# Six stationary buffers moved to six different offsets modulo 512 bytes

## The chip, the cores and the metric

The kernel runs on one core of one Trainium2 chip. The metric is the device time of one execution in microseconds; less is better. TensorE (PE) multiplies matrices, VectorE (DVE), ScalarE (ACT) and GpSimd (POOL) work element by element, and SyncE (SP) issues most of the loads from device memory.

## The reference

Two decoder layers act on x of 256 tokens by 2048 features, in float32. Layer 0 mixes tokens by gated linear attention, layer 1 by softmax attention with a forget gate, and both end in a SwiGLU network. In short:

```
for i in range(DEPTH):                       # DEPTH = 2
    h = rms_norm(x, norm_mix[i])
    x = x + (gla_mixer if i == 0 else fox_mixer)(h, ...)   # h @ w_in, mixing, (...) @ w_o
    h = rms_norm(x, norm_ffn[i])
    x = x + (silu(h @ w_gate) * (h @ w_up)) @ w_down       # 2048 -> 5632 -> 2048
```

Nearly all of the arithmetic lies in the products of 256 token rows with large weight matrices, which are read from device memory once.

## The kernel before

**The split.** Each float32 operand of a large product is split into a high part and a low part, both of type float32r. A product is then the sum of three: high by high, high by low, low by high. The weights stream in as chunks of 256 rows by 512 columns: `raw` receives the chunk by DMA, ScalarE writes `w_hi` from it (line 551), VectorE writes `w_lo` (line 890). Each of these three is a ring of 4 slots.

**The stationary buffers.** The activations are transposed and stand in pairs: `xt_hi` and `xt_lo` (the normed x, 16 blocks of 128 features by 256 tokens), `ht_hi` and `ht_lo` (the inner SwiGLU activations, 44 blocks) and `yt_hi` and `yt_lo` (a mixer's output, 16 blocks). One block holds 1024 bytes on each partition, and a matmul takes half of it, 128 tokens or 512 bytes, as its stationary operand. The weights are the moving operand, 512 columns or 2048 bytes. This is the inner loop of `tile`, lines 328 to 337:

```
for r in range(KC_CHUNK):                                     # 2
    k = j * KC_CHUNK + r
    wh = w_hi[:, slot, r * N:(r + 1) * N]                     # N = 512
    wl = w_lo[:, slot, r * N:(r + 1) * N]
    for b in range(TB):                                       # 2
        xh, xl = hi[:, k, b * P:(b + 1) * P], lo[:, k, b * P:(b + 1) * P]
        pe.matmul(o, xh, wh, start=(k == 0), stop=False)      # L335
        pe.matmul(o, xh, wl, start=False, stop=False)         # L336
        last = pe.matmul(o, xl, wh, start=False, stop=...)    # L337
```

There are 816 chunks of 12 such matmuls each. The trace names a matmul `acc<-w_hi,xt_hi`: it writes `acc` in PSUM and reads those two tensors. The weight load of the stationary operand is a separate instruction, LDWEIGHTS, with a row of its own ("PEld"). The second argument of `pe.matmul` is the stationary operand, the third the moving one.

**The narrow products.** Once in each layer, `narrow_product` multiplies the normed x with 16 further columns of the input weights, and there the roles are turned round: the stationary operand is a window of 128 columns into a narrow weight array, and x is the moving operand with 256 columns.

```
for k in range(KC):                                           # 16
    wh, wl = hi[:, k * R:k * R + P], lo[:, k * R:k * R + P]   # R = 16
    pe.matmul(wk[:, 0, 0:S], wh, xt_hi[:, k, :], ...)         # L347
    pe.matmul(wk[:, 0, 0:S], wh, xt_lo[:, k, :], ...)         # L348
    last = pe.matmul(wk[:, 0, 0:S], wl, xt_hi[:, k, :], ...)  # L349
```

**Where things lie.** A first pad brings `xres` to a multiple of 2048 bytes, and `xres`, `xt_hi`, `xt_lo`, `raw`, `w_hi` and `w_lo` follow without gaps, each 16384 bytes long, so all of them begin at multiples of 2048. Then come small tensors, and from `base`, again a multiple of 2048, a region in which the mixers' tensors and `ht`, `yt` take turns (function `at`, with offsets in units of 1024 bytes).

**The order of work.** Each engine's program is written out by hand, and semaphores join them. On TensorE the tiles follow one another; transposes of activations (line 305) and the small products of the mixers (lines 435 to 515) are slipped in between chunks. Nothing in this order depends on addresses.

Of the kernel before, what the change touches and what calls it, by code (L numbers as in the profile page):

```python
# [31 lines left out]
F32R = mybir.dt.float32r  # L32
# [5 lines left out]
P = 128  # L38
# [37 lines left out]
def build(nc, x, norm_mix, norm_ffn, gla_w_in, gla_w_g2, gla_b_g2, gla_o_gain, gla_w_o,  # L76
          fox_w_in, fox_b_f, fox_q_gain, fox_k_gain, fox_w_o, w_gate, w_up, w_down, out):
    S, D = x.shape[1], x.shape[2]
    KC = D // P
# [4 lines left out]
    HC = DFF // P  # L84
# [31 lines left out]
    with ctx:  # L116
        def sb(name, shape, dt=F32):
            return ctx.enter_context(nc.sbuf_tensor(name, shape, dt))
# [3 lines left out]


        ALIGN = 2048
        sb("pad", [P, (-(-(-nc.sbuf_base // 32) * 32)) % ALIGN // 4])
        xres = sb("xres", [P, TB, D])
        xt_hi = sb("xt_hi", [P, KC, S], F32R)
        xt_lo = sb("xt_lo", [P, KC, S], F32R)
        raw = sb("raw", [P, SLOTS, KC_CHUNK * N])
        w_hi = sb("w_hi", [P, SLOTS, KC_CHUNK * N], F32R)  # L130
        w_lo = sb("w_lo", [P, SLOTS, KC_CHUNK * N], F32R)
# [17 lines left out]
        ohr = sb("o_rstd", [P, GH, TB])  # L149


        base = -(-nc.sbuf_base // ALIGN) * ALIGN
        room = [0]

        def at(name, shape, offset, dt=F32):
            size = 4 * int(np.prod(shape[1:]))
            room[0] = max(room[0], offset + size)
            return nc.alloc_sbuf_tensor_at(name, shape, dt, offset=base + offset)
        K = 1024
        ht_hi = at("ht_hi", [P, HC, S], 0, F32R)  # L160
        ht_lo = at("ht_lo", [P, HC, S], 44 * K, F32R)
        yt_hi = at("yt_hi", [P, KC, S], 0, F32R)
        yt_lo = at("yt_lo", [P, KC, S], 16 * K, F32R)

        qT = at("gla_qT", [P, GF, S], 0)
        kT = at("gla_kT", [P, GF, S], 8 * K)
# [1249 lines left out]
```

## Time and profile before

| | |
|---|---|
| median of 3 runs | 2388.08 us (2388.03 to 2390.64) |
| the profiled execution | 2389.47 us, of which the span from first to last instruction is 2387.8 us |
| PE busy | 2364.1 us, 99% of the span, 10882 matmuls |
| weight loads (PEld) busy | 1965.7 us, 82% |
| DVE, ACT, POOL busy | 1256.1 us, 1070.0 us, 156.9 us |
| mean granted TensorE clock | 0.999 of full speed |

Matmuls overlap in the array, and their ends are modelled. So a row's duration of one matmul (some 390 ns) is longer than the distance between two starts; the distance is what an added matmul costs, and it is read from start times.

### The profile page before, as it was taken

The page shows a single profiled execution, that of the slowest core. Times are in us where ns is not written, and L with a number is a line of the kernel's source. Part 1 is how long each engine was busy: PE and PEld are TensorE (multiplying, and loading weights), DVE is VectorE, ACT ScalarE, POOL GpSimd, SP SyncE. Part 2 cuts the span into 40 slices and gives each one's busy share as a digit, 9 for nine tenths or more (in the row PEclk, how much of TensorE's full clock was granted, in tenths as well). Part 3 has the DMA queues.
Part 4 walks back from the last instruction along what each step waited for, and adds up shares of the span by engine and source line. Part 5 has one row for each costly group of instructions (what it writes and reads, how often), then busy time and mean ns, then how long its engine had stood idle before and what let it go on. Part 6 is the DMA issues. An engine that isn't in the chain of part 4 may idle for free.

```text
span 2387.8 us, 30464 instructions
## 1 busy us (share of the span) xinstructions
PE 2364.1 (99%) x10882; PEld 1965.7 (82%) x10882; DVE 1256.1 (53%) x1210; ACT 1070.0 (45%) x1242; POOL 156.9 (7%) x188
## 2 busy tenths in 40 slices
PE   8999999999999999999999999999999999999999
PEld 6788878888888888888888888888888888888887
DVE  4668655555445454444465555555454454444443
ACT  5544555444444444444444455444444444444332
POOL 2213210000000000000011110000000000000000
PEclk9999999999999999999999999999999999999999
DMA  6455455565665655566878786655665665656664
GB/s 206 133 168 159 143 166 185 189 191 184 193 193 181 193 189 186 193 190 188 195 165 185 179 212 162 157 176 189 192 190 187 191 191 187 188 182 196 206 200 138
DMA packets 228184, 435.39 MB, mean 182 GB/s; under 512 B 17444, under 2 KB 17544, under 8 KB 227992
## 3 DMA queue, kind: packets, MB, share of 16 engines
q1 hardware_dynamic: 223040, 429.97, 60.9%
q0 software_dynamic: 752, 4.21, 0.5%
q10 hardware_dynamic: 4328, 0.37, 0.1%
q8 instruction: 38, 0.62, 0.1%
q14 instruction: 26, 0.21, 0.0%
HBM read 432.38 MB, written 2.11 MB: 182 GB/s over the span
## 4 chain that ended last, share of the span: by engine, by line
PE 98%; DVE 1%; ACT 0%; DMA 0%; issue 0%; POOL 0%; DVEq 0%; ACTq 0%
PE acc L335 31%; PE acc L337 31%; PE acc L336 31%; PE tp L305 2%; PE wk L435 1%; DVE w_lo L890 1%; PE wk L487 0%; PE tp L497 0%; DMA xres<-in_x_dram 0%; PE wk L409 0%; PE wk L348 0%; PE wk L349 0%; PE wk L347 0%; PE wk L513 0%; PE wk L515 0%; PE wk L514 0%
## 5 line engine op out<-in xcount | busy, mean ns | idle before, releaser
L890 DVE TENSOR_TENSOR w_lo<-raw,w_hi 128x1024 fp32r<-128x1024 f32 x816 | 1029.9, 1272 | 885.9 <-ACT w_hi L551 885.3
L551 ACT ACTIVATE w_hi<-raw 128x1024 fp32r<-128x1024 f32 x816 | 861.0, 1060 | 1020.8 <-PE acc L337 956.1
L335 PE MATMUL acc<-w_hi,xt_hi 128*128 128x512 f32 x2304 | 907.4, 394 | 6.4 <-DVE gla_kT L1020 3.1
L337 PE MATMUL acc<-w_hi,xt_lo 128*128 128x512 f32 x2304 | 899.1, 390 | 0.0
L336 PE MATMUL acc<-w_lo,xt_hi 128*128 128x512 f32 x2304 | 898.6, 390 | 0.0
L335 PEld LDWEIGHTS acc<-w_hi,xt_hi 128*128 128x128 f32 x2304 | 433.7, 188 | 97.8 <-issue 5.6
L337 PEld LDWEIGHTS acc<-w_hi,xt_lo 128*128 128x128 f32 x2304 | 433.4, 188 | 90.7
L336 PEld LDWEIGHTS acc<-w_lo,xt_hi 128*128 128x128 f32 x2304 | 433.9, 188 | 89.0 <-issue 1.0
L335 PE MATMUL acc<-w_hi,ht_hi 128*128 128x512 f32 x704 | 274.6, 390 | 0.0
L337 PE MATMUL acc<-w_hi,ht_lo 128*128 128x512 f32 x704 | 274.2, 389 | 0.0
L336 PE MATMUL acc<-w_lo,ht_hi 128*128 128x512 f32 x704 | 274.1, 389 | 0.0
L337 PEld LDWEIGHTS acc<-w_hi,ht_lo 128*128 128x128 f32 x704 | 132.2, 188 | 27.5
L335 PEld LDWEIGHTS acc<-w_hi,ht_hi 128*128 128x128 f32 x704 | 132.2, 188 | 27.2
L336 PEld LDWEIGHTS acc<-w_lo,ht_hi 128*128 128x128 f32 x704 | 132.2, 188 | 27.1
L335 PE MATMUL acc<-w_hi,yt_hi 128*128 128x512 f32 x256 | 100.5, 393 | 0.0
L337 PE MATMUL acc<-w_hi,yt_lo 128*128 128x512 f32 x256 | 99.8, 390 | 0.0
L336 PE MATMUL acc<-w_lo,yt_hi 128*128 128x512 f32 x256 | 99.7, 389 | 0.0
L1305 POOL COPY xres<-stage 128x1024 f32<-128x1024 f32 x12 | 12.5, 1042 | 1067.9 <-DVE stage L923 1067.9
L305 PEld LDWEIGHTS tp<-ident,stage 128*128 128x128 f32 x432 | 50.3, 140 | 8.9 <-issue 2.0
L305 PE MATMUL tp<-ident,stage 128*128 128x128 f32 x432 | 56.0, 273 | 1.6 <-DVE stage L981 1.6
L337 PEld LDWEIGHTS acc<-w_hi,yt_lo 128*128 128x128 f32 x256 | 48.1, 188 | 10.0
L336 PEld LDWEIGHTS acc<-w_lo,yt_hi 128*128 128x128 f32 x256 | 48.1, 188 | 9.7
(173 smaller groups left out, 888.8 us busy)
## 6 DMA issues: line engine op xcount, KB each, us to landing
raw<-in_ffn_w_gate_dram SPq DMA_DIRECT2D x176, 512.0 KB, 4.3
raw<-in_ffn_w_up_dram SPq DMA_DIRECT2D x176, 512.0 KB, 4.3
raw<-in_ffn_w_down_dram SPq DMA_DIRECT2D x176, 512.0 KB, 4.5
raw<-in_fox_w_in_dram SPq DMA_DIRECT2D x128, 512.0 KB, 5.5
raw<-in_gla_w_in_dram SPq DMA_DIRECT2D x96, 512.0 KB, 4.1
raw<-in_gla_w_o_dram SPq DMA_DIRECT2D x32, 512.0 KB, 4.5
raw<-in_fox_w_o_dram SPq DMA_DIRECT2D x32, 512.0 KB, 4.5
xres<-in_x_dram SPq DMA_DIRECT2D x4, 512.0 KB, 7.9
```

Of the source, the lines that this page charges most:

```text
L305: last = pe.transpose(tp[:, kk, b * P:(b + 1) * P], src[:, b, kk * P:(kk + 1) * P], ident[:, :])
L335: pe.matmul(o, xh, wh, start=(k == 0), stop=False)
L336: pe.matmul(o, xh, wl, start=False, stop=False)
L337: last = pe.matmul(o, xl, wh, start=False, stop=(k == chunks * KC_CHUNK - 1))
L435: last = pe.matmul(wk[:, b, h * P:(h + 1) * P], ks, qs, start=(kf == 0), stop=(kf == FPH - 1))
L551: nc.scalar.activation(w_hi[:, slot, :], raw[:, slot, :], ACT.Copy).then_inc(hi_done, 1)
L890: nc.vector.tensor_tensor(w_lo[:, slot, :], raw[:, slot, :], w_hi[:, slot, :].bitcast(F32), ALU.subtract).then_inc(lo_done, 1)
L1305: nc.gpsimd.tensor_copy(xres[:, :, t * N:(t + 1) * N], stage[:, :, :]).then_inc(x_saved, 1)
```

## The change

The stationary buffers no longer begin at multiples of 512 bytes but at six different offsets modulo 512: `xt_hi` 64, `xt_lo` 256, `ht_hi` 128, `ht_lo` 320, `yt_hi` 192, `yt_lo` 448. `xres` stays where it was. `raw`, `w_hi` and `w_lo` move by 2048 bytes and stay at multiples of 2048. `base` becomes the next multiple of 512 instead of 2048, which moves the mixers' tensors by 512 bytes. No instruction is added, removed or reordered: on each of the five engines the program has the same rows in the same order, with other addresses.

```
         ALIGN = 2048
-        sb("pad", [P, (-(-(-nc.sbuf_base // 32) * 32)) % ALIGN // 4])
+        XT_HI_AT, XT_LO_AT = 64, 256
+        HT_HI_AT, HT_LO_AT = 128, 320
+        YT_HI_AT, YT_LO_AT = 192, 448
+
+        def to(name, align, offset):
+
+            start = -(-nc.sbuf_base // 32) * 32
+            gap = (offset - start) % align
+            if gap:
+                sb(name, [P, gap // 4])
+        to("pad_xres", ALIGN, 0)
         xres = sb("xres", [P, TB, D])
+        to("pad_xt_hi", 512, XT_HI_AT)
         xt_hi = sb("xt_hi", [P, KC, S], F32R)
+        to("pad_xt_lo", 512, XT_LO_AT)
         xt_lo = sb("xt_lo", [P, KC, S], F32R)
+        to("pad_raw", ALIGN, 0)
         raw = sb("raw", [P, SLOTS, KC_CHUNK * N])
         w_hi = sb("w_hi", [P, SLOTS, KC_CHUNK * N], F32R)
         w_lo = sb("w_lo", [P, SLOTS, KC_CHUNK * N], F32R)
...
-        base = -(-nc.sbuf_base // ALIGN) * ALIGN
+        base = -(-nc.sbuf_base // 512) * 512
...
         K = 1024
-        ht_hi = at("ht_hi", [P, HC, S], 0, F32R)
-        ht_lo = at("ht_lo", [P, HC, S], 44 * K, F32R)
-        yt_hi = at("yt_hi", [P, KC, S], 0, F32R)
-        yt_lo = at("yt_lo", [P, KC, S], 16 * K, F32R)
+        ht_hi = at("ht_hi", [P, HC, S], HT_HI_AT, F32R)
+        ht_lo = at("ht_lo", [P, HC, S], 44 * K + HT_LO_AT, F32R)
+        yt_hi = at("yt_hi", [P, KC, S], YT_HI_AT, F32R)
+        yt_lo = at("yt_lo", [P, KC, S], 16 * K + YT_LO_AT, F32R)
```

## Rows read from the trace of the kernel before

**Rows 1.** the page: busy time by engine, then the granted clock in 40 slices.
```profile
PE 2364.1 (99%) x10882; PEld 1965.7 (82%) x10882; DVE 1256.1 (53%) x1210; ACT 1070.0 (45%) x1242; POOL 156.9 (7%) x188
...
PEclk9999999999999999999999999999999999999999
```

**Rows 2.** the page: the chain that ended last, by engine, by line.
```profile
PE 98%; DVE 1%; ACT 0%; DMA 0%; issue 0%; POOL 0%; DVEq 0%; ACTq 0%
PE acc L335 31%; PE acc L337 31%; PE acc L336 31%; PE tp L305 2%; PE wk L435 1%; DVE w_lo L890 1%; PE wk L487 0%; PE tp L497 0%; DMA xres<-in_x_dram 0%; PE wk L409 0%; PE wk L348 0%; PE wk L349 0%; PE wk L347 0%; PE wk L513 0%; PE wk L515 0%; PE wk L514 0%
```

**Rows 3.** the page: TensorE by line (busy, mean ns of one | idle before).
```profile
L335 PE MATMUL acc<-w_hi,xt_hi 128*128 128x512 f32 x2304 | 907.4, 394 | 6.4 <-DVE gla_kT L1020 3.1
...
L336 PE MATMUL acc<-w_lo,xt_hi 128*128 128x512 f32 x2304 | 898.6, 390 | 0.0
L335 PEld LDWEIGHTS acc<-w_hi,xt_hi 128*128 128x128 f32 x2304 | 433.7, 188 | 97.8 <-issue 5.6
...
L335 PE MATMUL acc<-w_hi,ht_hi 128*128 128x512 f32 x704 | 274.6, 390 | 0.0
...
L335 PE MATMUL acc<-w_hi,yt_hi 128*128 128x512 f32 x256 | 100.5, 393 | 0.0
```

**Rows 4.** whom TensorE waited for: total us, times, longest.
```profile
PE tp L305 <- DMA xres<-in_x_dram: 5.5, 1, 5.5
PE tp L305 <- DVE xt_lo L931: 4.6, 1, 4.6
PE acc L335 <- DVE gla_kT L1020: 3.1, 1, 3.1
PE acc L335 <- DVE w_lo L890: 3.1, 2, 2.5
```

**Rows 5.** line 336 in three unbroken stretches: count, then first and last start.
```profile
L336 PE MATMUL acc<-w_lo,xt_hi x64: 386/389/390, 1974.2 to 2017.1; 128*128 128x512 f32 x64
...
L336 PE MATMUL acc<-w_lo,yt_hi x32: 387/390/391, 357.7 to 378.8; 128*128 128x512 f32 x32
...
L336 PE MATMUL acc<-w_lo,ht_hi x310: 388/389/390, 2159.9 to 2370.0; 128*128 128x512 f32 x155
```

**Rows 6.** timeline, first narrow product: start us, us, instruction.
```profile
39.81 0.28 PE L347 MATMUL wk<-xt_hi,gla_wn_hi 128*128 128x256 f32 x1
...
40.16 0.28 PE L347 MATMUL wk<-xt_hi,gla_wn_hi 128*128 128x256 f32 x1
...
40.52 0.28 PE L347 MATMUL wk<-xt_hi,gla_wn_hi 128*128 128x256 f32 x1
...
40.87 0.28 PE L347 MATMUL wk<-xt_hi,gla_wn_hi 128*128 128x256 f32 x1
...
41.23 0.28 PE L347 MATMUL wk<-xt_hi,gla_wn_hi 128*128 128x256 f32 x1
...
41.58 0.28 PE L347 MATMUL wk<-xt_hi,gla_wn_hi 128*128 128x256 f32 x1
...
41.94 0.28 PE L347 MATMUL wk<-xt_hi,gla_wn_hi 128*128 128x256 f32 x1
...
42.30 0.28 PE L347 MATMUL wk<-xt_hi,gla_wn_hi 128*128 128x256 f32 x1
...
42.65 0.28 PE L347 MATMUL wk<-xt_hi,gla_wn_hi 128*128 128x256 f32 x1
...
43.01 0.28 PE L347 MATMUL wk<-xt_hi,gla_wn_hi 128*128 128x256 f32 x1
...
45.14 0.28 PE L347 MATMUL wk<-xt_hi,gla_wn_hi 128*128 128x256 f32 x1
```

**Rows 7.** pieces of the chain: start us, us, what.
```profile
8.82 1.57 ACT xt_hi L595 x4
10.49 1.67 DVE xt_lo L931 x4
...
149.99 3.57 PE wk L435 x32
```

## The prediction

> **What bounds the kernel now.** I read the page from the top. TensorE is busy for 99% of the span and its granted clock is full, the upper of its two levels (2.4 GHz), in all slices [rows 1]. Such a busy share proves little, because the ends of matmuls are modelled. So I turn next to the chain of work that ended last: 98% of it is TensorE, and three lines of the inner loop, 335, 336 and 337, hold 31% each [rows 2]. No other engine decides anything for long. The list of TensorE's waits confirms it: the longest are 5.5 us for the first piece of x, 4.6 us for `xt_lo`, and twice 3.1 us in the first layer [rows 4], 16.3 us in all. The kernel is a stream of matmuls, and its time is their number times the distance from one start to the next.
>
> The number comes from the code, 816 chunks of 12, and from the rows by line: each of the three lines ran 2304 times with `xt`, 704 times with `ht` and 256 times with `yt` [rows 3], and 3 x 3264 is 9792. The distance comes from stretches in which nothing is slipped between the chunks. Line 336 is every third matmul there. With `xt` 64 of them lie between 1974.2 and 2017.1 us, so 42.9 / 63 / 3 = 227.0 ns a matmul; with `yt` 32 lie in 21.1 us, 226.9 ns; with `ht` 310 lie in 210.1 us, 226.6 ns [rows 5]. I take 226.8 ns. All three kinds pay the same within the rounding of the starts, and 9792 x 226.8 ns is 2220.8 us, 93% of the span of 2387.8 us. The rest, 167.0 us, is transposes, the mixers' small products and the waits.
>
> One nanosecond on each of these matmuls is 9.8 us, or 0.41%. About 0.2% (4.8 us) is what a measurement of this kernel can tell from no change, and that is 0.49 ns a matmul. The question is thus a fine one: does the address of the stationary operand move that distance by half a nanosecond?
>
> **What could be there to gain.** The narrow products, with 256 columns, start every 118.4 ns (worked out below). So 256 more columns cost 108.4 ns, 0.423 ns each, which is about one cycle of 2.4 GHz (0.417 ns). 512 such cycles are 213.3 ns, the distance is 226.8, and so 13.5 ns a matmul is something else. If the weight load and the moving stream got in each other's way, and if that depended on both starting at multiples of 512 bytes, this is where the change would act. The weight load takes 188 ns [rows 3] and so lies within the distance of 226.8 ns, beside the matmul before it. An offset that made only the load shorter would be covered by the 38.8 ns between the two, and bring nothing. An offset that made it longer would bring nothing either up to those 38.8 ns.
>
> **What the trace of before already tried.** The narrow product is the same experiment, on a small scale. Its stationary windows begin at k times 64 bytes in an array that begins at a multiple of 2048, so k = 0 to 7 run through all eight multiples of 64 modulo 512, the changed kernel's 64, 128, 192, 256, 320 and 448 among them. Its moving operand begins at a multiple of 512, as the ring does. Three matmuls make a step k. From the start of k = 0 to the start of k = 8 the steps of line 347 are 0.35, 0.36, 0.35, 0.36, 0.35, 0.36, 0.36 and 0.35 us, the next is 0.36, and 15 steps take 5.33 us [rows 6]: 355.3 ns a step, 118.4 ns a matmul. No residue stands out. If leaving the multiple of 512 took away most of the 13.5 ns, the steps between k = 0 and k = 8 would be up to 40 ns shorter than those at k = 0 and 8. They are not, by 10 ns in three matmuls, or 3.3 ns in one.
>
> The two kinds of product give the fixed part as well. At 0.423 ns a column, 512 columns take 216.8 ns of the 226.8, which leaves 10.0 ns. At one cycle of 2.4 GHz a column the fixed parts are 13.5 ns in the large products and 118.4 - 106.7 = 11.7 ns in the narrow ones. Either way a matmul whose stationary operand is off the multiple of 512 pays nearly all of what an aligned one pays.
>
> **The change part by part.**
> - The offsets of `xt`, `ht` and `yt` as stationary operands: 9792 matmuls. The value taken is 0 ns, since the eight residues of the narrow product cannot be told apart. The bound of the gain is the difference of the fixed parts, 1.8 ns or 17.6 us. The bound of the loss is the spread of the narrow steps, 3.3 ns or 32.6 us.
> - The ring moves by 2048 bytes and keeps its place modulo 2048: 0. Its slots already differ by 4096 bytes, and the matmuls keep their pace over all four.
> - `xt` as the moving operand of the narrow products, now off the multiple of 512: 96 matmuls. If each lost the whole fixed part of 10.0 ns again, it would be 1.0 us. Taken as 0.
> - The mixers' tensors move by 512 bytes. Their blocks already lie at 512-byte steps from each other; 32 small products of line 435 over such blocks take 3.57 us [rows 7], 111.6 ns each, and the groups of that line have all steps in them. Taken as 0; a tenth of it, for the 272 of that line, would be 3.0 us.
> - ScalarE's and VectorE's writes into the six buffers begin elsewhere. They are hidden behind TensorE, as these engines are busy 45% and 53% of the span [rows 1], except for the start, where four of `xt_hi` (1.57 us) and four of `xt_lo` (1.67 us) stand in the chain [rows 7], once more before the first chunk. If they took a tenth more or less, that would be 0.6 us. Taken as 0.
> - `yt_lo` now reaches 448 bytes into what follows it. The program's waits are the same, and the tensors there are used at other times, so nothing comes later.
>
> The sum is 0. The profiled execution took 2389.47 us, 1.67 us more than its span; the median of the runs is 1.39 us below it, and with no change the forecast is that median, **2388.1 us**.
>
> **Two pages weighed.** The 226.8 ns of [rows 5] stand against a page's figure. The Trainium skill, "TensorE: Matmul & The Clock Gate", section "Wait — 56ns, not 53.3ns?", gives 215.7 ns for back-to-back matmuls of 512 columns at the full clock. If the offsets brought this kernel there, the time would be an estimated 2388.1 - 9792 x 11.1 ns = 2279 us by that page. The trace does not agree with that figure here. The Trainium skill, "SBUF — State Buffer", section "Who interferes with whom", speaks against any such gain: TensorE has two independent read ports, one for the moving operand and one for the weight load, so the two have nothing to collide on. By that rule the time stays at 2388.1 us, and the even steps of [rows 6] agree.
>
> **The rivals.**
> - *Slower, by straddling.* An aligned 512-byte stationary operand lies within one block of 512 bytes; at an offset it lies in two. If the array's load then delays each matmul by a little, all 9792 pay. For it: the first narrow step, which begins with an aligned operand, takes 0.35 us and the mean step 355.3 ns, 5.3 ns in three or 1.8 ns in one. Against it: steps of 0.35 us come back at k = 2, 4 and 7, and the weight load has 38.8 ns of cover. Price: 9792 x 1.8 ns = 17.6 us, 2405.7 us; by the bound of 3.3 ns, 2420.7 us. It decides from 0.49 ns a matmul.
> - *Faster a little.* The fixed part falls from 13.5 to the narrow product's 11.7 ns. For it: that difference is in the rows. Against it: those matmuls have 256 columns, and the difference may come from that. Price: 17.6 us, 2370.5 us; half of it, 2379.3 us.
> - *Faster by much.* There is a collision, which the narrow product does not leave either, because `wn` and `x` share something else. Price: the fixed part of 10.0 ns at most, 97.9 us, 2290.2 us. Against it: even steps over all residues.
>
> **How the numbers follow.** No change has a chance of 0.64, slower by straddling 0.20, faster a little 0.12, faster by much 0.04. Within the first, the time is 2388.1 us give or take 4.8 us, 2383 to 2393. The two small rivals are steps of about one nanosecond or less as easily as of 1.8, so the range takes in half of each: down to the 2379 us of half the small gain, and up to 1.2 ns of loss, 2400 us. What is left out is the large gain, 0.04, a part of the small one, 0.05, and the losses above, 0.09.
>
> **What would show it.** Line 336 in the same stretches must again have 226.6 to 227.0 ns from start to start; a weight load of 188 ns that changed while the distance did not would prove the cover. Steps of the narrow product must stay at 355 ns. `xt`, `ht` and `yt` have different offsets, so if one residue matters, the three will part: that would make the prediction wrong in a way the three stretches show at once. A common shift of all three by more than 0.5 ns would refute it as well.

## The result and the profile after

The changed kernel is slower: 2437.2 us median (2437.0 to 2438.7) against 2388.06 us, a ratio of 1.0205 with a 95% interval of 1.019 to 1.022, or 49 us. The forecast was no change, 2388.1 us, in a range of 2379 to 2400.

The page of the changed kernel: busy times, granted clock, chain by engine, then TensorE by line. Its inner loop stands 13 lines lower, at 348 to 350.

```profile
PE 2413.1 (99%) x10882; PEld 1963.5 (81%) x10882; DVE 1255.8 (52%) x1210; ACT 1070.7 (44%) x1242; POOL 156.7 (6%) x188
...
PEclk9999999999999999999999999999999999999999
...
PE 98%; DVE 1%; ACT 0%; DMA 0%; issue 0%; POOL 0%; DVEq 0%; ACTq 0%
...
L348 PE MATMUL acc<-w_hi,xt_hi 128*128 128x512 f32 x2304 | 916.4, 398 | 4.9 <-DVE w_lo L903 3.4
...
L349 PE MATMUL acc<-w_lo,xt_hi 128*128 128x512 f32 x2304 | 909.6, 395 | 0.0
L348 PEld LDWEIGHTS acc<-w_hi,xt_hi 128*128 128x128 f32 x2304 | 433.0, 188 | 109.6 <-DVE w_lo L903 4.5
```

Against [rows 1] and [rows 2] nothing but TensorE's busy time has grown, by 49.0 us; clock and chain are the same. The weight load still takes 188 ns, as in [rows 3]. What has risen is the modelled duration of one matmul, from 394 to 398 ns on the first line and from 390 to 395 on the second. TensorE's waits (total us, times, longest) are no longer either:

```profile
PE tp L318 <- DMA xres<-in_x_dram: 5.6, 1, 5.6
PE tp L318 <- DVE xt_lo L944: 4.6, 1, 4.6
PE acc L348 <- DVE w_lo L903: 3.4, 3, 2.5
...
PE acc L348 <- DVE gla_kT L1033: 1.5, 1, 1.5
```

These four are 15.1 us, against 16.3 us in [rows 4]. So no wait has come in. What has changed is seen in unbroken stretches of line 349, the middle matmul of three: count, then first and last start in us. The first two are `xt`, in a late SwiGLU and in the first layer's projections (the product with `w_in`), then come `yt` and `ht`.

```profile
L349 PE MATMUL acc<-w_lo,xt_hi x63: 390/390/397, 1785.9 to 1829.3; 128*128 128x512 f32 x63
...
L349 PE MATMUL acc<-w_lo,xt_hi x32: 396/397/398, 86.3 to 107.8; 128*128 128x512 f32 x32
...
L349 PE MATMUL acc<-w_lo,yt_hi x31: 388/388/388, 385.0 to 405.6; 128*128 128x512 f32 x31
...
L349 PE MATMUL acc<-w_lo,ht_hi x351: 388/394/394, 2187.6 to 2429.1; 128*128 128x512 f32 x176
```

By the same working as for [rows 5]: 43.4 us / 62 / 3 is 233.3 ns from start to start for `xt`, 21.5 us / 31 / 3 is 231.2 ns in the projections, `yt` has 20.6 / 30 / 3 or 228.9 ns, and `ht` 241.5 / 350 / 3 or 230.0 ns. Before, all had 226.7, in ns. Of the changed kernel's 33 stretches of `xt` with 60 matmuls or more, 29 run at 233.3 ns, and four, three of them in the first layer's projections, at 231.1. The 49 us are there. Summed over all matmuls of the two traces, from start to start, those with `xt` took 40.9 us more, those with `ht` 7.0 us (2112 x 3.3 ns) and those with `yt` 1.7 us (768 x 2.2 ns), 49.5 us together. TensorE's few pauses came out 2.1 us shorter, nothing else moved by more than 0.2 us, and the span grew by 47.5 us.

A closer look, at the timeline of single matmuls in the projections (start us, modelled duration, instruction):

```profile
60.11 0.39 PE L348 MATMUL acc<-w_hi,xt_hi 128*128 128x512 f32 x1
60.34 0.40 PE L349 MATMUL acc<-w_lo,xt_hi 128*128 128x512 f32 x1
60.57 0.39 PE L350 MATMUL acc<-w_hi,xt_lo 128*128 128x512 f32 x1
60.80 0.39 PE L348 MATMUL acc<-w_hi,xt_hi 128*128 128x512 f32 x1
61.03 0.40 PE L349 MATMUL acc<-w_lo,xt_hi 128*128 128x512 f32 x1
61.26 0.39 PE L350 MATMUL acc<-w_hi,xt_lo 128*128 128x512 f32 x1
61.50 0.39 PE L348 MATMUL acc<-w_hi,xt_hi 128*128 128x512 f32 x1
```

Two rounds of three matmuls take 1.39 us (60.11 to 61.50), 231.7 ns each within the rounding, and the middle one of each three is modelled at 0.40 us where its neighbours have 0.39. It is a settled rhythm, not a scatter of delays: in ns the distances repeat 226, 236, 232 in the projections, and in the SwiGLU stages a pattern of six with a mean of 233.3. Written in cycles of 2.4 GHz the mean distances are 544 before and 554.7, 560, 549.3 and 552 after: thirty-four steps of 16 cycles before, and 34 2/3, 35, 34 1/3 and 34 1/2 after. What is whole is the pattern: three matmuls take 104 or 103 steps, six take 210 or 207. A step of 16 cycles is 6.67 ns, an estimated 16 columns at the 0.423 ns a column of the prediction, and 16 columns are 64 bytes on a partition.

### The profile page after: what moved, and what is told of

Same layout as the page of the kernel before. It is cut to its first block, busy times and chain, and to the rows that moved or that the text cites. A ratio compares the mean times of both kernels' runs of the same rounds, so it can differ in the third digit from the quotient of the medians.

```text
span 2435.3 us, 30464 instructions
## 1 busy us (share of the span) xinstructions
PE 2413.1 (99%) x10882; PEld 1963.5 (81%) x10882; DVE 1255.8 (52%) x1210; ACT 1070.7 (44%) x1242; POOL 156.7 (6%) x188
## 4 chain that ended last, share of the span: by engine, by line
PE 98%; DVE 1%; ACT 0%; DMA 0%; issue 0%; POOL 0%; DVEq 0%; ACTq 0%
PE acc L350 31%; PE acc L348 31%; PE acc L349 31%; PE tp L318 2%; PE wk L448 1%; DVE w_lo L903 1%; PE wk L500 0%; PE tp L510 0%; DMA xres<-in_x_dram 0%; PE wk L422 0%; PE wk L361 0%; PE wk L360 0%; PE wk L362 0%; PE wk L527 0%; PE wk L528 0%; PE wk L526 0%
## 5 line engine op out<-in xcount | busy, mean ns | idle before, releaser
L350 PE MATMUL acc<-w_hi,xt_lo 128*128 128x512 f32 x2304 | 912.3, 396 | 0.0
L349 PE MATMUL acc<-w_lo,xt_hi 128*128 128x512 f32 x2304 | 909.6, 395 | 0.0
```

The source lines that it names most:

```text
L350: last = pe.matmul(o, xl, wh, start=False, stop=(k == chunks * KC_CHUNK - 1))
```

## Experiments

In all of them the order of instructions is that of the kernel before, TensorE writes to the same places in PSUM, and a weight load takes 188 to 189 ns. Three kinds of matmul (`xt`, `ht`, `yt`) can have different offsets, so one kernel tries three at once. "Offset" is a place in bytes modulo 2048 for `xt` and the ring (all of `raw`, `w_hi`, `w_lo`, unless said otherwise), and modulo 512 for the others. The distance from start to start is worked out as above; with starts rounded to 0.1 us it is good to 0.5 ns for `xt`, 1 ns for `yt` and 0.1 ns for `ht`, and where this text gives a number of steps of 16 cycles or speaks of a settled distance, it is from the trace's starts in ns, after the first 24 matmuls of a stretch. The diffs are against the changed kernel and leave out its own lines; where two kernels share one, the second's values stand behind it. Where there is one timed run, its time is given as it stands: the kernel before, run beside them, took 2387.9 to 2391.0 us.

**Are equal offsets free?** (e1, against the changed kernel)

```
-        XT_HI_AT, XT_LO_AT = 64, 256
-        HT_HI_AT, HT_LO_AT = 128, 320
-        YT_HI_AT, YT_LO_AT = 192, 448
+        XT_HI_AT, XT_LO_AT = 64, 64
+        HT_HI_AT, HT_LO_AT = 256, 256
+        YT_HI_AT, YT_LO_AT = 128, 128
```

> High and low part of a pair at the same offset modulo 512: xt 64 and 64, ht 256 and 256, yt 128 and 128; ring at multiples of 2048. Theory A (each stationary operand that is off the multiple of 512 costs by itself, by crossing a boundary): all three kinds stay above the 226.7 ns from start to start of the kernel before, at 229 to 234 ns, and the time stays at 2410 to 2440 us. Theory B (what costs is that the two parts of a pair have different offsets, so that successive weight loads begin differently): all three return to 226.7 ns, time 2388 us. Theory C (what counts is the offset from the moving operand's): as A, with three different distances.

Measured: 2435.53 us, ratio 1.0195 (1.0178 to 1.0212). Line 349 with `xt`, `yt` and `ht`:

```profile
L349 PE MATMUL acc<-w_lo,xt_hi x63: 394/394/394, 1788.0 to 1831.4; 128*128 128x512 f32 x63
...
L349 PE MATMUL acc<-w_lo,yt_hi x31: 390/393/404, 387.1 to 408.0; 128*128 128x512 f32 x31
...
L349 PE MATMUL acc<-w_lo,ht_hi x351: 389/389/395, 2189.6 to 2427.6; 128*128 128x512 f32 x176
```

`xt` has 43.4 / 62 / 3, 233.3 ns; `yt` 232.2 (settled at 232.4); `ht`, with 238.0 us from first to last start, 238.0 / 350 / 3 or 226.7 ns. Theory B falls: equal parts at 64 and at 128 pay as much as unequal ones, and those of `xt` alone bring most of the loss of the changed kernel. Theory A falls in its plain form too, because 256 is free.

**Only one part moved** (e3)

```
+        XT_HI_AT, XT_LO_AT = 64, 0
+        HT_HI_AT, HT_LO_AT = 0, 64
+        YT_HI_AT, YT_LO_AT = 256, 512
```

> Only one part of each pair is off the multiple of 512: xt 64 and 0, ht 0 and 64, yt 256 and 0 (at 512). Two of three matmuls load the high part, one the low part. Theory A: the cost goes with the number of matmuls off the multiple, so xt and yt lose twice what ht loses; with some 6.6 ns a matmul for a full pair of xt, xt 231 ns and ht 229 ns. Theory B (a change of offset between successive loads costs): xt and ht lose alike, since both change offset twice in three matmuls. Time 2410 to 2425 us by either.

Measured: 2437.58 us. Two stretches with `xt`, then `yt`, then `ht`:

```profile
L349 PE MATMUL acc<-w_lo,xt_hi x63: 397/397/398, 453.3 to 496.3; 128*128 128x512 f32 x63
...
L349 PE MATMUL acc<-w_lo,xt_hi x63: 390/390/397, 1785.3 to 1828.7; 128*128 128x512 f32 x63
...
L349 PE MATMUL acc<-w_lo,yt_hi x31: 389/389/389, 385.0 to 405.4; 128*128 128x512 f32 x31
...
L349 PE MATMUL acc<-w_lo,ht_hi x351: 388/392/392, 2187.0 to 2429.6; 128*128 128x512 f32 x176
```

`xt` has 231.2 ns in one stretch and 233.3 in another, `ht` 231.0 (settled at 231.1), `yt` 226.7. One part off is nearly as dear as both, so the cost does not go with the number of matmuls off the multiple, as A had it. And matmuls with the same operand addresses can settle in two rhythms. They are the two of `xt` in the changed kernel, 231.1 and 233.3 ns: its offsets there, 64 and 256, are those of this run, 64 and 0, if 256 counts as 0.

**Does it matter where in 2048?** (e4)

```
+        XT_HI_AT, XT_LO_AT = 512, 1024      # xt pads modulo 2048
+        HT_HI_AT, HT_LO_AT = 0, 1024        # base is 512 modulo 2048
+        YT_HI_AT, YT_LO_AT = 512, 1024
```

> All six at multiples of 512 but at different places modulo 2048: xt 512 and 1024, ht 512 and 1536, yt 1024 and 1536. Theories A, B and C, which all count modulo 512: 226.7 ns for all, 2388 us, as the blocks of a buffer lie at steps of 512 in the kernel before too. A theory D, by which the pad to 2048 matters: above 226.7 ns in at least one kind, over 2395 us.

Measured: 2387.84 us, the time before. With `xt` 226.9 ns, with `ht` 226.7:

```profile
L349 PE MATMUL acc<-w_lo,xt_hi x63: 387/389/389, 447.5 to 489.7; 128*128 128x512 f32 x63
...
L349 PE MATMUL acc<-w_lo,ht_hi x351: 389/389/389, 2141.9 to 2379.9; 128*128 128x512 f32 x176
```

So the larger footprint, the ring 2048 bytes further on and the mixers' tensors 512 bytes further on, all of which this kernel shares with the changed one, cost nothing. The whole 49 us come from the offsets below 512.

**The stationary's address, or its distance from the ring?** (e2 and e7)

```
+        XT_HI_AT, XT_LO_AT = 0, 0           # e2          e7: 192, 192
+        HT_HI_AT, HT_LO_AT = 64, 64         #                  0, 0
+        YT_HI_AT, YT_LO_AT = 128, 128       #                 64, 64
-        to("pad_raw", ALIGN, 0)
+        to("pad_raw", ALIGN, 64)            #                 192
...
+        to("pad_stage", 512, 0)             # both
```

> The ring (raw, w_hi, w_lo) begins at 64 modulo 2048; xt at 0 and 0, ht at 64 and 64, yt at 128 and 128. Theory A (offset of the stationary operand alone): xt 226.7 ns from start to start, ht and yt above it, about 2395 to 2405 us. Theory C (offset of the stationary from the moving operand): ht, which lies as far from the ring as before, has 226.7 ns, while xt and yt are above, about 2420 to 2435 us. Theory B (unequal parts): 226.7 ns in all three, 2388 us.

Measured: 2408.84 us. `xt`, `yt` and `ht`:

```profile
L350 PE MATMUL acc<-w_lo,xt_hi x63: 388/388/388, 1768.6 to 1811.2; 128*128 128x512 f32 x63
...
L350 PE MATMUL acc<-w_lo,yt_hi x31: 393/398/398, 384.3 to 405.3; 128*128 128x512 f32 x31
...
L350 PE MATMUL acc<-w_lo,ht_hi x351: 389/389/389, 2162.9 to 2400.9; 128*128 128x512 f32 x176
```

> Ring at 192 modulo 2048, xt at 192 and 192, ht at 0 and 0, yt at 64 and 64. Theory C256 (offset from the ring counts): xt, off every multiple of 256 but level with the ring, has the 226.7 ns of the kernel before; ht, aligned but 64 above the ring modulo 256, has 233.3; yt, 128 from it, some 233. Time about 2403 us. Theory A (the stationary operand's own address counts): xt 228.9 ns, ht 226.7, yt 233.3, about 2405 us; the two differ by which kind pays.

Measured: 2406.04 us. `xt`, `yt` and `ht`:

```profile
L350 PE MATMUL acc<-w_lo,xt_hi x63: 389/389/395, 1762.4 to 1804.6; 128*128 128x512 f32 x63
...
L350 PE MATMUL acc<-w_lo,yt_hi x31: 390/393/404, 380.6 to 401.5; 128*128 128x512 f32 x31
...
L350 PE MATMUL acc<-w_lo,ht_hi x351: 393/398/398, 2153.1 to 2398.1; 128*128 128x512 f32 x176
```

These two runs separate A from C. In the first, `ht` stands off every multiple of 256 and is free (238.0 / 350 / 3 = 226.7 ns), because the ring is moved as far; `xt`, aligned but 64 below the ring, pays 229.0 ns. In the second, `xt` at 192 is level with the ring and has 226.9 ns, and `ht`, perfectly aligned, pays 233.3 ns. Theory C holds, in so far as the place against the ring counts, and theory A is dead. That `raw` moves with the ring is not the reason: in e8, below, `w_lo` alone is moved, and aligned `yt` goes from 226.7 to 232 ns.

**Modulo what, and how much for each offset?** (e5 and e6; ring at 0)

```
+        XT_HI_AT, XT_LO_AT = 192, 192       # e5          e6: 224, 224
+        HT_HI_AT, HT_LO_AT = 32, 32         #                 96, 96
+        YT_HI_AT, YT_LO_AT = 320, 320       #                160, 160
```

> Pairs at equal offsets, ring at multiples of 2048: xt 192, ht 32, yt 320. Theory C256 (the offset of the stationary from the moving operand counts modulo 256, as 0 gave 226.7 ns, 64 and 128 some 233, -64 gave 228.9 and 256 gave 226.7): yt at 320 behaves as 64, 233.3 ns; xt at 192 behaves as -64, 228.9 ns; ht at 32, not measured before, between 226.7 and 233.3. Theory C512 (modulo 512, and 256 is free by chance): yt at 320 = -192 and xt at 192 have distances of their own, not 233.3 and 228.9. Time by C256 about 2400 to 2410 us.

Measured: 2420.47 us. `xt`, `yt` and `ht`:

```profile
L349 PE MATMUL acc<-w_lo,xt_hi x63: 388/388/388, 1773.4 to 1815.9; 128*128 128x512 f32 x63
...
L349 PE MATMUL acc<-w_lo,yt_hi x31: 393/393/398, 383.0 to 404.0; 128*128 128x512 f32 x31
...
L349 PE MATMUL acc<-w_lo,ht_hi x351: 395/396/396, 2167.5 to 2412.5; 128*128 128x512 f32 x176
```

> Pairs at equal offsets, ring at multiples of 2048: xt 224 (that is -32 modulo 256), ht 96, yt 160. Theory C256 with a cost that falls back evenly beyond 128: xt between 226.7 and 228.9 ns, yt between 228.9 and 233, ht 233. A rival: there is an offset below the aligned one's 226.7 ns, which is two 16-cycle steps above 512 cycles; then xt, at -32, is the place for it, with 220 ns, and the time falls under 2370 us.

Measured: 2451.65 us. `xt`, `yt` and `ht`:

```profile
L349 PE MATMUL acc<-w_lo,xt_hi x63: 393/396/397, 1796.1 to 1839.5; 128*128 128x512 f32 x63
...
L349 PE MATMUL acc<-w_lo,yt_hi x31: 388/394/394, 387.0 to 408.0; 128*128 128x512 f32 x31
...
L349 PE MATMUL acc<-w_lo,ht_hi x351: 392/397/400, 2197.7 to 2443.7; 128*128 128x512 f32 x176
```

By its rows `xt` has 228.5 ns, within the rounding of the 229.0 in e2. The offset 320 gives the 233.3 ns of 64, and 192 the 229 of -64 in e2, as 256 gave the 226.7 of 0 in e1: the count is modulo 256 wherever it was tried. The guess that the cost falls back evenly beyond 128 is wrong, since 160 and 224 cost 233.3 ns as 64 does. So is the hope for a place below the aligned one. With both parts alike, and the offset counted from the ring modulo 256, these are the settled distances, with the number of matmuls after which the pattern of distances repeats:

| offset from the ring | ns from start to start | steps of 16 cycles | repeats after | from |
|---|---|---|---|---|
| 0 (also 256) | 226.7 | 34 | 1 | e1, e2, e3, e4, e7, e10 |
| 32 | 233.3 | 35 | 2 | e5 |
| 64 (also 320) | 233.3 | 35 | 1 or 2 | e1, e2, e5, e7 |
| 96 | 234.3 | 35 1/7 | 7 | e6 |
| 128 | 232.4 | 34 6/7 | 7 | e1, e7 |
| 160 | 233.3 | 35 | 3 | e6 |
| 192 (-64) | 228.9 | 34 1/3 | 3 | e2, e5 |
| 224 | 233.3 | 35 | 4 | e6 |

The kernel before has 226.7 ns as well, its single distances scattered between 225 and 228 ns. The rhythm of a row is that of most of its stretches, not of all: one stretch of `xt` in the first projections of e5, at 192, ran at 233.3 ns.

The changed kernel's `yt`, 192 and 448, is two times 192 by this count, and its 228.9 ns are those of the table.

**A version that keeps all at multiples of 256** (e10)

```
+        XT_HI_AT, XT_LO_AT = 256, 0
+        HT_HI_AT, HT_LO_AT = 256, 512
+        YT_HI_AT, YT_LO_AT = 768, 1280
-        to("pad_raw", ALIGN, 0)
+        to("pad_raw", 512, 0)
         raw = sb("raw", [P, SLOTS, KC_CHUNK * N])
+        to("pad_w_hi", 512, 0)
         w_hi = sb("w_hi", [P, SLOTS, KC_CHUNK * N], F32R)
+        to("pad_w_lo", 512, 256)
```

> Everything that TensorE reads in the large products begins at a multiple of 256 bytes, and no two the same way modulo 2048 if it can be had: xt 256 and 512, ht 1792 and 0, yt 256 and 768, w_hi 512, w_lo 768. Theory C256: 226.7 ns for all three kinds and the time of the kernel before, 2388 us, within 0.2%. Theory C512 or a rule of 2048: one or more kinds above 228 ns and over 2395 us.

Measured: 2388.27 us, ratio 1.000 (0.9991 to 1.001). `xt`, `yt` and `ht`, all at 226.7 to 226.9 ns:

```profile
L351 PE MATMUL acc<-w_lo,xt_hi x63: 387/389/389, 449.3 to 491.5; 128*128 128x512 f32 x63
...
L351 PE MATMUL acc<-w_lo,yt_hi x31: 389/389/389, 381.3 to 401.7; 128*128 128x512 f32 x31
...
L351 PE MATMUL acc<-w_lo,ht_hi x351: 387/389/389, 2143.7 to 2381.8; 128*128 128x512 f32 x176
```

The rule of 2048 in the kernel before is stricter than needed; 256 does, for the stationary and the moving operands.

**Which pair collides?** (e8 and e11: `w_lo` alone at 64)

```
+        XT_HI_AT, XT_LO_AT = 0, 64          # e8         e11: 64, 0
+        HT_HI_AT, HT_LO_AT = 0, 64          #                 64, 64
+        YT_HI_AT, YT_LO_AT = 0, 0           #                128, 192
+        to("pad_w_lo", ALIGN, 64)           # both
```

> w_hi at 0 and w_lo at 64 modulo 2048; xt 0 and 64, ht 0 and 64, yt 0 and 0. The weight load of the next matmul runs beside the stream of the one before: high part beside w_hi (line 337's stream loads the next high part), high beside w_hi again, low beside w_lo. Theory N (the load collides with the stream it runs beside): xt and ht have no offset in any such pair and keep 226.7 ns, although low parts and w_lo are off the multiple; yt pays in one of three. Theory S (the stationary operand collides with its own matmul's moving operand): xt and ht have a difference of 64 in two of three matmuls and pay, 229 to 233 ns. Time by N about 2388 to 2392 us, by S about 2420 to 2440 us.

Measured: 2429.89 us. `xt`, `yt` and `ht`:

```profile
L351 PE MATMUL acc<-w_lo,xt_hi x63: 394/394/394, 1781.2 to 1824.2; 128*128 128x512 f32 x63
...
L351 PE MATMUL acc<-w_lo,yt_hi x31: 388/395/398, 384.6 to 405.5; 128*128 128x512 f32 x31
...
L351 PE MATMUL acc<-w_lo,ht_hi x351: 388/394/397, 2179.2 to 2421.9; 128*128 128x512 f32 x176
```

> w_hi at 0, w_lo at 64; xt 64 and 0, ht 64 and 64, yt 128 and 192. By theory S (each matmul's own pair counts, taken from 226.7, 233.3 and 228.9 ns for 0, 64 and -64): xt has the pairs 64, 0, 0 and a mean of 228.9 ns; ht has 64, 0, 64 and 231.1 ns. By theory N (the load beside the stream before it): xt 64, -64, 64 and 231.8 ns, ht 64, 0, 64 and 231.1 ns. By a theory M (any offset that differs between what is read next and what was read before it costs, as xt and ht paid 231.1 ns with w_lo at 64): xt and ht both near 231 ns or above.

Measured: 2453.91 us. `xt` and `ht`:

```profile
L351 PE MATMUL acc<-w_lo,xt_hi x63: 393/396/398, 1752.5 to 1795.9; 128*128 128x512 f32 x63
...
L351 PE MATMUL acc<-w_lo,ht_hi x351: 388/398/400, 2199.8 to 2445.9; 128*128 128x512 f32 x176
```

In e8 `xt` and `ht` pay 231.1 to 231.2 ns where theory N wanted 226.7, and `yt`, with both parts aligned, settles at 232.0, although by either theory only one of its three matmuls has an offset: at 6.6 ns for that one, the mean would be 228.9. In e11 `xt` pays 233.3 and `ht` 234.4 (246.1 / 350 / 3), where S wanted 228.9 and 231.1, and N 231.8 and 231.1. Neither sum over single pairs gives these. Theory M, that any difference among what is read costs, is what is left, and it says little. Which two reads get in each other's way stays open.

**Offsets under 32 bytes** (e12)

```
+        def late(t, blocks, by):
+            return t[:, by // 4:by // 4 + blocks * S].rearrange("p (k s) -> p k s", s=S)
...
+        xt_hi = late(sb("xt_hi", [P, KC * S + 64], F32R), KC, 16)     # xt_lo alike
+        ht_hi = late(at("ht_hi", [P, HC * S + 64], HT_HI_AT, F32R), HC, 240) # HT_HI_AT = 0; ht_lo alike
+        yt_hi = late(at("yt_hi", [P, KC * S + 64], YT_HI_AT, F32R), KC, 8)   # YT_HI_AT = 0; yt_lo alike
```

> Offsets finer than the allocator's 32 bytes, through views into larger tensors: both parts of xt 16 bytes past a multiple of 512, ht 240 (16 before a multiple of 256), yt 8; ring at multiples of 2048. If every mismatch costs in the large products: all three kinds above 226.7 ns, some 230 to 235, time 2410 to 2440 us. If there is a place with less than the aligned distance, as the narrow product has one at 64 (117.8 against 119.8 ns), it can only lie between the offsets tried: one kind then falls to 224 ns or less, and the time of that kind below that of the kernel before.

Measured: 2423.52 us. Two neighbouring stretches with `xt`, then `yt`, then `ht` in the second layer and in the first:

```profile
L352 PE MATMUL acc<-w_lo,xt_hi x63: 394/394/394, 1779.4 to 1822.8; 128*128 128x512 f32 x63
...
L352 PE MATMUL acc<-w_lo,xt_hi x63: 389/389/389, 1734.3 to 1776.5; 128*128 128x512 f32 x63
...
L352 PE MATMUL acc<-w_lo,yt_hi x31: 391/392/397, 386.8 to 407.6; 128*128 128x512 f32 x31
...
L352 PE MATMUL acc<-w_lo,ht_hi x351: 389/389/397, 2177.6 to 2415.6; 128*128 128x512 f32 x176
...
L352 PE MATMUL acc<-w_lo,ht_hi x88: 387/391/392, 952.6 to 1012.2; 128*128 128x512 f32 x88
```

At 16 bytes `xt` runs at 233.3 ns in one stretch and at 226.7 in the one before it, with the same code and the same addresses; these are turns of one loop, and its turns go 233.3, 226.7, 233.3, 233.3, 226.7 and so on. `ht` at 240 has two rhythms as well: 226.7 in the second layer and in two of four stretches of the first, and 59.6 / 87 / 3 or 228.4 ns in the other two. `yt` at 8 has 231.1 by its row and settles at 230.7. Nothing is below the aligned distance. After each interruption by transposes TensorE settles anew, and at 16 and at 240 it has two rhythms to settle in.

**Why did the narrow product show nothing?** (e9, against the kernel before; the narrow products here multiply with other windows of the narrow weights, so their values are others)

```
-                    wh, wl = hi[:, k * R:k * R + P], lo[:, k * R:k * R + P]
+                    at_ = (k // 8 * 8 if which == 0 else k // 8 * 8 + 1) * R
+                    wh, wl = hi[:, at_:at_ + P], lo[:, at_:at_ + P]
```

> The kernel before, except that the narrow products read other windows of the narrow weights, so their result is another one: in the first layer every window begins at a multiple of 512 bytes, in the second every one begins 64 bytes past it. If the law of the large products (64 off costs one step of 16 cycles, 6.7 ns a matmul) held in the narrow products too, the first has about 5 to 7 ns a matmul less than the second, 113 against 120 ns instead of 118.3 in both, and the even steps of the kernel before were an average over the offsets. If the narrow products are bound by something else, for example by their weight loads, which take 188 ns against a distance of 118 ns, both stay at 118 to 119 ns and the narrow product was no test of the question at all. Time 2388 us, as 96 matmuls weigh nothing.

Measured: 2390.92 us. The timeline of line 348, each row being one step of three matmuls: first layer (all windows at multiples of 512), two rows 14 steps apart, then second layer (all windows 64 bytes past a multiple of 512), two rows 11 steps apart:

```profile
40.24 0.28 PE L348 MATMUL wk<-xt_hi,gla_wn_hi 128*128 128x256 f32 x1
...
45.28 0.28 PE L348 MATMUL wk<-xt_hi,gla_wn_hi 128*128 128x256 f32 x1
...
1352.42 0.28 PE L348 MATMUL wk<-xt_hi,fox_wn_hi 128*128 128x256 f32 x1
...
1356.30 0.28 PE L348 MATMUL wk<-xt_hi,fox_wn_hi 128*128 128x256 f32 x1
```

Aligned, 14 steps take 5.04 us, 120.0 ns a matmul, 18 steps of 16 cycles. At an offset of 64, 11 steps take 3.88 us, 117.6 ns a matmul; from the starts in ns it is 117.8, 17 2/3 steps of 16 cycles, and the difference is 2.2 ns. In the kernel before both layers had 118.3 ns, so the layer makes no difference. The offset does matter in the narrow product, then, but with the other sign and a third of the size. Neither expectation had that.

## Why the prediction was wrong

- **What bounds the kernel** held: the loss lies in the distance of the 9792 matmuls, with no new wait and no other engine. That one nanosecond a matmul is 9.8 us held as well; the loss of 49 us is some 5 ns.
- **The step that failed** is "The value taken is 0 ns, since the eight residues of the narrow product cannot be told apart", and before it "The narrow product is the same experiment, on a small scale". It is not the same experiment. e9 shows that in the narrow product an offset of 64 makes a matmul 2.2 ns shorter, where in the large ones it makes it 6.6 ns longer (e1). In place of the 0 ns the changed kernel paid 6.6 ns with `xt` in most stretches, 3.3 with `ht` and 2.2 with `yt`. An operation with 256 columns started every 118 ns, while weight loads of 188 ns overlap one another, does not speak for one with 512 columns started every 227 ns.
- **The even steps were read too strongly.** Each step of the narrow product has another offset than the last. The runs show that a stream of one kind settles in a rhythm of up to seven matmuls, once of fifteen, and e12 that it can take either of two. A walk through eight offsets, three matmuls each, may settle in none. In the trace of before, read in ns, steps with the same offset differ: 359 and 352 ns at k = 6 and 14, 355 and 359 at k = 4 and 12. So its mean of 118.4 ns need be no offset's settled rate, and by e9 it is neither the 120.0 nor the 117.8. Nor could rows of 0.01 us show the difference of those two, 7 ns a step.
- **The bound of the loss**, 3.3 ns a matmul from the spread of the narrow steps, was a bound for the wrong product: the large ones lost up to 6.6 ns.
- **The cover** was reasoned as if only the load's length could change. The load's 188 ns did not change; the distance did. The 38.8 ns between the two protected nothing.
- **The rival "slower, by straddling"** had the right side and the wrong mechanism, and its highest price, 32.6 us, is below the 49 us measured. In e7 `ht` lies within one block of 512 bytes and pays, and `xt` straddles and doesn't. What counts is the place of the stationary operands against the ring, modulo 256.
- **The page that spoke for no effect.** The Trainium skill, "SBUF — State Buffer", section "Who interferes with whom", gives TensorE two independent read ports. e2 and e7 don't agree with what the prediction concluded from it, that the two have nothing to collide on: moving the ring alone against a stationary buffer changes the distance by 2.2 to 6.6 ns. Whether that happens at the memory or in the array's own sequencing, no run tells.
- **The other parts of the change** were rightly costed at nothing: e4 shares the moves of the ring and of the mixers' tensors and has the time before. The writes into the moved buffers and the narrow products cost nothing either: outside the large matmuls nothing of TensorE's time grew by more than 0.1 us, and the narrow products have 118.8 ns a matmul after, 118.3 before.
- **What would show it** was right: the three kinds parted, at 233.3, 230.0 and 228.9 ns, in the three stretches named.

What stays open: which two reads interfere, since e8 and e11 fit neither sum of pairs; why the narrow products and the large ones have opposite signs, as not only the columns but the roles of the two operands differ; and whether the 32 cycles that aligned operands pay over one a column can be had back by anything else than an offset. No offset tried went below 34 steps, so there is no version here that beats the kernel before.

## What to carry to other kernels

Put everything that TensorE reads in its large products, stationary and moving, at the same place modulo 256 bytes; multiples of 256 are the simple way, and an offset of 32 or 64 between the two cost 3% of each matmul here. Check it by the distance between matmul starts in an unbroken stretch, not by busy shares or by the length of the weight load, which did not move. And do not take a rate from a short run of another shape in which the condition changes at every step.

## What the runs showed of the hardware

- The settled distances between float32r matmuls of 128 by 128 by 512 repeat after a few matmuls, and each pattern takes a whole number of steps of 16 cycles at 2.4 GHz (6.67 ns): 34 or 35 for one, 103, 104 or 105 for three, 137 for four and 173 for five (e12), 207, 209, 210 or 211 for six, 244 or 246 for seven (e1, e6).
- The distance depends on the stationary operand's address less the moving operand's, modulo 256 bytes: it is 226.7 ns at 0 and 2.2 to 7.6 ns longer at the multiples of 32 tried, where both parts of a pair lie alike.
- The same code at the same addresses can settle at two rates, 226.7 and 233.3 ns at an offset of 16 bytes, 226.7 and 228.3 ns at 240. With the high part alone at 64 matmuls with the same operand addresses had 231.1 and 233.3 ns.
- In the narrow products, of 256 columns, the aligned case is the slower one, 120.0 against 117.8 ns at an offset of 64 (e9).
